# Expert loop of a one-core mixture block: transposes inside the down products, a later dispatch, 2 MB weight transfers

## The reference, cut to what matters

```python
logits = (t @ w_router + b_router)             # t: (512, 1024)
top_val, top_idx = lax.top_k(logits, 4)
gate = jax.nn.softmax(top_val, axis=-1)
# for every expert e, on the tokens routed to it
h = xb @ w_mlp1[e] + b_mlp1[e]                 # (n, 1024) @ (1024, 2048)
glu, lin = jnp.split(h, 2, axis=-1)
glu = jnp.minimum(glu, 7.0)
lin = jnp.clip(lin, -7.0, 7.0)
a = glu * jax.nn.sigmoid(1.702 * glu) * (lin + 1)
y = a @ w_mlp2[e] + b_mlp2[e]                  # (n, 1024) @ (1024, 1024)
out[token] += y * gate                         # then residual and a final RMS norm
```

## Time and profile before

| | |
|---|---|
| median of 3 runs | 1647.25 us (1645.18 to 1649.3) |
| the profiled execution's own time | 1645.66 us |
| its span | 1643.8 us |
| first product of the expert loop | 566.07 us |
| last product of the expert loop | ends at 1610.61 us |
| PE, busy and share of the span | 1437.5 us, 87% |
| DVE, ACT, POOL | 757.7, 546.1, 293.5 us |
| bytes moved | 475.18 MB |

### The profile page before, as it was taken

The page is one execution under the profiler, slowest core; times in us unless marked ns, Lnnn a source line. Parts: engine busy times, 40 slices in busy tenths (PEclk is TensorE's granted clock), DMA queues, the critical chain, the costliest instruction groups (busy, mean ns, idle before and its releaser), DMA issues. The chain is left out here.

```text
span 1643.8 us, 36064 instructions
## 1 busy us (share of the span) xinstructions
PE 1437.5 (87%) x13229; PEld 765.6 (47%) x13230; DVE 757.7 (46%) x1812; ACT 546.1 (33%) x1035; POOL 293.5 (18%) x188
## 2 busy tenths in 40 slices
PE   5899998599997688899999899889889898898981
PEld 2788875366776233344444334333333333343431
DVE  6899976899314623322233233323422422332236
ACT  3432223655323022333223322332342333223323
POOL 4344557411461000000000000000000000000000
PEclk8999998799999699999999999999999999999996
DMA  4223231111329289999999999999999999999995
GB/s 152 77 89 102 90 103 41 37 39 39 106 93 381 96 322 401 411 386 371 373 373 408 404 401 409 396 406 399 413 412 391 412 410 404 409 397 391 404 406 206
DMA packets 78112, 475.18 MB, mean 289 GB/s; under 512 B 11008, under 2 KB 11264, under 8 KB 28928
## 3 DMA queue, kind: packets, MB, share of 16 engines
q1 hardware_dynamic: 69648, 455.72, 70.1%
q0 software_dynamic: 7280, 16.79, 2.9%
q10 hardware_dynamic: 1152, 2.24, 0.4%
HBM read 466.71 MB, written 16.78 MB: 294 GB/s over the span
## 5 line engine op out<-in xcount | busy, mean ns | idle before, releaser
L1033 PE MATMUL bank<-big,ring 128*32 128x512 f32 x4992 | 562.3, 605 | 49.0 <-issue 48.9
L1033 PEld LDWEIGHTS bank<-big,ring 128*32 128x32 f32 x4992 | 156.9, 111 | 420.8 <-issue 419.8
L1055 PE MATMUL bank<-big,mix 128*32 128x256 f32 x4992 | 279.1, 380 | 0.7 <-DMA big<-in_d_w 0.7
L992 ACT ACTIVATE mix<-bank,sgate 32x256 f32<-32x256 f32 x384 | 179.2, 467 | 157.4 <-PE bank L1055 123.8
L1055 PEld LDWEIGHTS bank<-big,mix 128*32 128x32 f32 x4992 | 157.4, 110 | 107.9 <-issue 4.7
L957 POOL DMA_INDIRECT y_rows<-mix,sidx x32 | 30.9, 965 | 914.3 <-ACT mix L992 914.3
L981 ACT ACTIVATE ring<-ring 128x256 f32<-128x256 f32 x96 | 40.1, 417 | 439.4 <-DVE ring L1178 439.4
L1176 DVE TENSOR_TENSOR ring<-bank,b 128x512 f32<-128x512 f32 x96 | 66.1, 688 | 202.7 <-PE bank L1033 196.4
L435 PE MATMUL bank<-mix_r,sm_r 128*128 128x512 f32 x344 | 141.6, 412 | 15.5 <-POOL uT_r L234 10.1
L673 DVE SCALAR_TENSOR_TENSOR bank<-big,chan,bank 128x512 f32<-128x512 f32 x224 | 148.2, 752 | 0.0
L435 PE MATMUL bank<-uT_r,sm_r 128*128 128x512 f32 x344 | 136.6, 397 | 0.0
(11 more groups left out here) (262 smaller groups left out, 1649.7 us busy)
## 6 DMA issues: line engine op xcount, KB each, us to landing
big<-in_d_w SPq DMA_DIRECT2D x384, 1024.0 KB, 16.2
ring<-in_d_dense SPq DMA_DIRECT2D x67, 512.0 KB, 3.3
big<-y_rows SPq DMA_DIRECT2D x2, 2048.0 KB, 22.3
xT<-in_d_xT SPq DMA_DIRECT2D x4, 512.0 KB, 9.3
uT<-in_d_x SPq DMA_DIRECT2D x1, 2048.0 KB, 9.6
u_rows<-xT SPq DMA_DIRECT2D x4, 512.0 KB, 16.6
xT<-y_rows SPq DMA_DIRECT2D x1, 2048.0 KB, 15.9
xT<-y_rows SPq DMA_DIRECT2D x4, 512.0 KB, 5.3
```

Of the source, the lines that this page charges most:

```text
L992: out = act.activation(t.ysb[g * G:(g + 1) * G, c * FC:(c + 1) * FC], bank[PY[g % 2]][token, 0:FC], ACT.Copy, scale=t.sgate[token, bass.ds ...
L1033: mm = pe.matmul(halves(bank[g][c * G:(c + 1) * G, :], FC), t.xe[:, k, g * G:(g + 1) * G], cols, start=(k == 0), stop=(k == KB - 1), tile_ ...
L1055: mm = pe.matmul(bank[PY[g % 2]][c * G:(c + 1) * G, 0:FC], t.aT[:, g, x, b * G:(b + 1) * G], t.w2[:, b, x, c * FC:(c + 1) * FC], start=(b ...
```

## The change

Six things, all in the expert loop.

1. `K_EACH` is 4 instead of 5.
2. `dispatch(i + 1)` and `spread_bias(i)` come after the second chunk of w1 instead of after the first.
3. `turn_act(i, 0)` stands before the last tile's second half of `up` in a three-tile piece, and after `up` in a two-tile piece; `turn_act(i, g + 1)` stands inside `down(i, g)`, after its third quarter.
4. The sequencer's waits with `sem_inc` of two-tile pieces give way to `after(sem)`, a matmul of one column whose end updates the semaphore.
5. DVE turns each tile right after its `swiglu`, and ACT copies the next piece's transposed rows after the second sigmoid instead of after the third.
6. The weights come in transfers of 2 MB: four for w1 and two for w2, each with a row of 16 KB per partition, laid out so in HBM. Chunks are released, and waited for, in pairs. The first expert's weights too.

```diff
-K_EACH = 5
+K_EACH = 4
+PAIRS = KB // 2
...
-                for k in range(KB):
-                    sp.wait_ge(t.s_w1used, i * KB + (k + 1 - KB))
-                    sp.dma_start(t.w1[:, k, :], t.d_w1[bass.ds(e, 1), k * P:(k + 1) * P, :].rearrange("a p n -> (a p) n")).then_inc(t.s_w1[k], 16)
-                for j in range(4):
-                    sp.wait_ge(t.s_w2used, i * 4 + (j - 3))
+                for q in range(PAIRS):
+                    sp.wait_ge(t.s_w1used, i * PAIRS + (q + 1 - PAIRS))
+                    sp.dma_start(t.w1[:, 2 * q:2 * q + 2, :], t.d_w1[bass.ds(e, 1), q].rearrange("e p a n -> (e p) a n")).then_inc(t.s_w1[q], 16)
+                for q in range(2):
+                    sp.wait_ge(t.s_w2used, i * 2 + (q - 1))
...
-                turn(i + 1)
+                    if g == 1:
+                        turn(i + 1)
...
+            def after(sem):
+
+                pe.matmul(bank[5][0:G, 2 * P:2 * P + 1], ident[:, 0:G], ident[:, 0:1], start=True, stop=True).then_inc(sem, 1)
+
...
-                    if g == 0:
-                        pe.wait_ge(t.s_w2[b], i * 16 + 16)
+                    if g == 0 and b % 2 == 0:
+                        pe.wait_ge(t.s_w2[b // 2], i * 16 + 16)
...
+                    if b == 2 and g < last:
+                        turn_act(i, g + 1)
+                        if g + 2 == NG - 1 and last < NG - 1:
+                            after(t.s_at)
...
-                    mm.then_inc(t.s_w1used, 1)
-                    if k == 0:
+                    if k % 2:
+                        mm.then_inc(t.s_w1used, 1)
+                    if k == 1:
                         pe.wait_ge(t.s_slots, i + 1)
                         pe.wait_ge(t.s_ysb, i * NG + 1)
                         dispatch(i + 1)
                         spread_bias(i)
                 for g in range(groups):
+                    if g == NG - 1:
+                        pe.wait_ge(t.s_slots, i + 3)
+                        turn_act(i, 0)
...
                 if groups < NG:
-
-                    pe.wait_ge(t.s_w1used, i * KB + KB)
-                    pe.sem_inc(t.s_up, 1)
-                pe.wait_ge(t.s_slots, i + 2)
-                turn_act(i, 0)
+                    pe.wait_ge(t.s_slots, i + 3)
+                    after(t.s_up)
+                    turn_act(i, 0)
                 turn(i + 1)
-                turn_act(i, 1)
                 down(i, 0, last)
-                if groups == NG:
-                    turn_act(i, 2)
-                else:
-                    pe.wait_ge(t.s_ae, i * NG + 3)
-                    pe.sem_inc(t.s_at, 1)
                 down(i, 1, last)
                 if groups == NG:
                     down(i, 2, last)
                 else:
-                    pe.wait_ge(t.s_w2used, i * 4 + 4)
-                    pe.sem_inc(t.s_y, 1)
+                    after(t.s_y)
...
-                for g in range(2):
+                for g in range(NG):
                     gated(i, g, step, base)
                     swiglu(i, g)
-                turned(i, 0)
-                gated(i, 2, step, base)
-                turn(i + 1)
-                turned(i, 1)
-                swiglu(i, 2)
-                turned(i, 2)
+                    if g == 1:
+                        turn(i + 1)
+                    turned(i, g)
```

More of the change, by code:

```diff
@@ L203, in _ @@
             sp.wait_ge(t.s_merge, 2 * KB)
-            for k in range(KB - 2):
-                sp.dma_start(t.w1[:, k, :], t.d_w1[0, k * P:(k + 1) * P, :]).then_inc(t.s_w1[k], 16)
-            for j in range(4):
-                sp.dma_start(t.w2[:, j, :, :], t.d_w2[0, j]).then_inc(t.s_w2[j], 16)
+            for q in range(PAIRS - 1):
+                sp.dma_start(t.w1[:, 2 * q:2 * q + 2, :], t.d_w1[0, q]).then_inc(t.s_w1[q], 16)
+            for q in range(2):
+                sp.dma_start(t.w2[:, 2 * q:2 * q + 2, :, :], t.d_w2[0, q]).then_inc(t.s_w2[q], 16)
             sp.wait_ge(t.s_prod, used(N_CHUNK - 1))
-            for k in range(KB - 2, KB):
-                sp.dma_start(t.w1[:, k, :], t.d_w1[0, k * P:(k + 1) * P, :]).then_inc(t.s_w1[k], 16)
+            sp.dma_start(t.w1[:, KB - 2:KB, :], t.d_w1[0, PAIRS - 1]).then_inc(t.s_w1[PAIRS - 1], 16)
             for j in range(TT):
@@ L920, in _ @@
                 e = expert_of(sp, i)
-                for k in range(KB):
-                    sp.wait_ge(t.s_w1used, i * KB + (k + 1 - KB))
-                    sp.dma_start(t.w1[:, k, :], t.d_w1[bass.ds(e, 1), k * P:(k + 1) * P, :].rearrange("a p n -> (a p) n")).then_inc(t.s_w1[k], 16)
-                for j in range(4):
-                    sp.wait_ge(t.s_w2used, i * 4 + (j - 3))
-                    sp.dma_start(t.w2[:, j, :, :],
-                                 t.d_w2[bass.ds(e, 1), j].rearrange("e p a n -> (e p) a n")).then_inc(t.s_w2[j], 16)
+                for q in range(PAIRS):
+                    sp.wait_ge(t.s_w1used, i * PAIRS + (q + 1 - PAIRS))
+                    sp.dma_start(t.w1[:, 2 * q:2 * q + 2, :], t.d_w1[bass.ds(e, 1), q].rearrange("e p a n -> (e p) a n")).then_inc(t.s_w1[q], 16)
+                for q in range(2):
+                    sp.wait_ge(t.s_w2used, i * 2 + (q - 1))
+                    sp.dma_start(t.w2[:, 2 * q:2 * q + 2, :, :],
+                                 t.d_w2[bass.ds(e, 1), q].rearrange("e p j a n -> (e p) j a n")).then_inc(t.s_w2[q], 16)
             sp.wait_ge(t.s_scat, last * 16)
@@ L931, in _ @@
                 if r:
-                    sp.wait_ge(t.s_w1used, last * KB + 2 * r)
+                    sp.wait_ge(t.s_w1used, last * PAIRS + r)
                 sp.dma_start(t.early[r], t.d_y4[:, :, r, :]).then_inc(t.s_early[r], 16)
@@ L988, in _ @@
                     else:
-                        act.wait_ge(t.s_w2used, i * 4 + 4)
+                        act.wait_ge(t.s_w2used, i * 2 + 2)
                     for c in range(4):
@@ L1056, in down @@
                                            start=(b == 0 and x == 0), stop=(b == 3 and x == 1), tile_position=(0, c * G))
-                    if g == last:
+                    if g == last and b % 2:
                         mm.then_inc(t.s_w2used, 1)
+                    if b == 2 and g < last:
+                        turn_act(i, g + 1)
+                        if g + 2 == NG - 1 and last < NG - 1:
+                            after(t.s_at)
                 if g < last:
@@ L1065, in work @@
                 for k in range(K_EACH):
-                    pe.wait_ge(t.s_w1[k], i * 16 + 16)
+                    if k % 2 == 0:
+                        pe.wait_ge(t.s_w1[k // 2], i * 16 + 16)
                     for g in range(groups):
                         mm = up(k, g)
-                    mm.then_inc(t.s_w1used, 1)
-                    if k == 0:
+                    if k % 2:
+                        mm.then_inc(t.s_w1used, 1)
+                    if k == 1:
                         pe.wait_ge(t.s_slots, i + 1)
@@ L1075, in work @@
                 for g in range(groups):
+                    if g == NG - 1:
+                        pe.wait_ge(t.s_slots, i + 3)
+                        turn_act(i, 0)
                     for k in range(K_EACH, KB):
-                        if g == 0:
-                            pe.wait_ge(t.s_w1[k], i * 16 + 16)
+                        if g == 0 and k % 2 == 0:
+                            pe.wait_ge(t.s_w1[k // 2], i * 16 + 16)
                         mm = up(k, g)
-                        if g == last:
+                        if g == last and k % 2:
                             mm.then_inc(t.s_w1used, 1)
@@ L1172, in gated @@
                 else:
-                    dve.wait_ge(t.s_w1used, i * KB + KB)
+                    dve.wait_ge(t.s_w1used, i * PAIRS + PAIRS)
                 if g == 0:
@@ L1498, in build @@
         t.s_w = sems("s_w", NSLOT)
-        t.s_w1 = sems("s_w1", KB)
-        t.s_w2 = sems("s_w2", 4)
+        t.s_w1 = sems("s_w1", PAIRS)
+        t.s_w2 = sems("s_w2", 2)
         t.s_early = sems("s_early", TOPK - 1)
@@ L1575, in lay_out @@
         "d_b2": np.tile(a["b_mlp2"][0], (TT, 1)), "d_b1": b1,
-        "d_w1": a["w_mlp1"][0],
-        "d_w2": a["w_mlp2"][0].reshape(E, 4, 2, P, D).transpose(0, 1, 3, 2, 4),
+        "d_w1": a["w_mlp1"][0].reshape(E, PAIRS, 2, P, 2 * D).transpose(0, 1, 3, 2, 4),
+        "d_w2": a["w_mlp2"][0].reshape(E, 2, 2, 2, P, D).transpose(0, 1, 4, 2, 3, 5),
     }
```

## The result

The changed kernel takes 1636.06 us (median of 7, 1633.0 to 1640.05), the kernel before 1645.18 in the same comparison (median of 7, 1641.81 to 1649.3). The ratio is 0.995, interval 0.9937 to 0.9964: faster by 0.5%, about 9 us, where 25 us were forecast. The profiled execution took 1639.19 us, span 1637.4. Its loop runs from 565.3 to 1602.9 us, 1037.6 us instead of 1044.5.

A forecast was written before the change was run, and what follows sets the result against it. TensorE looked like the bound, within about 1% of the transfers' pace, which then caps the gain. First product 566.1, +6.1, stream +998.5, +9.5, rows -5, gather +5, end +6.5 give 1586.7; with 33.2 and 1.9, 1622 us; range 1603 to 1643.

The forecast's parts named there:

- the term of the stream: Expert loop: weights, gather and scatter need 31 x 13.11 = 406.4 MB, 998.5 us at 407 GB/s.
- its idle time in the first piece: Stream in the loop's first piece: 41 us at 283 GB/s carry 28.5 us of work; +9.5 us charged.
- PE's gain: TensorE in the loop: 60 us idle and 10 us half clock go, 9 us of new matmuls come; 983 us alone.
- Larger rows: Weight transfers: 16 KB rows save between nothing and 27 us; 5 us taken.
- The gather behind larger rows: Two-tile pieces, before `turn(i + 1)`: the gather lands later, PE waits 0 to 3.0 us in 18 pieces; 5 us charged.
- The clock: Waits for weights in two-tile pieces bring half clock; up to 24 us in three-tile pieces, 1646 us; nothing charged; chance 0.06.
- Waits for weights: Expected sign in the loop: PE waits for `big<-in_d_w` 25 to 50 us in total instead of 2.
- The second rival: Late gather at full price in two-tile pieces: PE 983 + 54 = 1037 us, time 1638 us; chance 0.12.
- No gain: Stream was the bound already at 32.6 us per piece, 13 us more; later releases 10 us: 1645 us; chance 0.09.
- The stream is no wall: Weight stream: larger rows save their upper bound, 27 us instead of 5, giving 1600 us; chance 0.08.

The follow-up runs named there:

- without a stream: Weight transfers inside the loop cut to 64 bytes per partition: changed kernel 1581.54 us, kernel before 1644.28 us.
- the runs with one strip: One of four column strips computed in up and down, all transfers kept: changed kernel 1629.81 us, kernel before 1637.46 us.

## Why the prediction was wrong

**The step that failed** is the term of the stream, "998.5 us at 407 GB/s", with "its idle time in the first piece, +9.5". With the 5 us each for larger rows and the gather it came to 1008 us from the first issue to the last landing. Measured: 572.5 to 1597.0, 1024.5 us. The mechanism was right, the stream caps PE's gain; the term was too small by 16.5 of the 17.4 us between the sum and the profiled execution. The other 0.9 is small differences at both ends. The parts of the 16.5, worked out from the landings:

- The pace. A piece was put at 32.2 us, from the 407 GB/s of one window of 282.6 us. It is 32.5, of which the weights are 29.5 and gather and scatter 3.0. Over 31 pieces, +9. The 407 already contained gather and scatter, so their price is not what was missed; the window was too short to stand for the loop. In the same trace the last landings of experts 9 to 31 are 32.6 us apart, and a longer window has 404 GB/s, 32.4 us:

```profile
900.00:1550.00 650.00, 591.96 (x6880) 250.69 (x6876) 208.91 (x684) 210.95 (x405) 37.99 (x40) 0.98 1.00 404
```

- The run of three-tile pieces 4 to 7. PE needs 35.8 us there and the single buffer stops the stream; experts 7 to 9 took 36.6, 35.0 and 33.8 us: +8. The prediction says that the late release "costs nothing later as long as there is always a transfer queued", and there was not. With narrow matmuls these 8 us go. With 1 MB transfers they stand elsewhere: experts 7 to 9 take 97.9 us in all, but the first 45.2 and the next two 33.8 and 34.2, and the whole stream 1024.9 us.
- The first expert took 43.2 us, 10.7 over the pace instead of 9.5: +1. The last took 2 less, without gather and scatter in its way.

**Point by point.** *PE's gain*: 60 + 10 - 9 = 61 us predicted, 66.1 of loop and 62.7 of time measured without a stream. Right, and so are its places; two-tile pieces in a row kept 1.1 us before the dispatch, nine times. *Larger rows*: 5 us taken; 4.4 us in the old order, nothing beyond noise in the new one. In the runs with one strip the pace differed by 0.1 us per expert. The price of the row is not separated from that of the release in pairs, which works the other way. *The gather behind larger rows*: predicted landing 8.6 to 13.1 us after issue, measured 12.1; predicted wait 0 to 3.0 us per two-tile piece, measured 1.8 in the mean of 14, 2.7 at most. Charged 5 us; with 1 MB transfers the wait is gone and the time is 1 us less, since PE waits for weights instead. The Trainium skill ("DMA: Bandwidth & Descriptors", Queues, rings and completion order) has engines serve their queues in turn; the landing times agree, nearer the upper figure. *The clock*: it fell where forecast, in starved two-tile pieces (0.90, 28.56 us busy instead of 24.72), and the three-tile pieces after the first kept 1.00. In the loop PE is busy 933 us instead of the 909 without a stream; nothing was charged for it. That fits the stream as the bound, but no run tests the clock by itself. *Waits for weights*: 25 to 50 us predicted, 16.2 measured, 40.2 with 1 MB transfers.

**The rivals.** The second rival's time, 1638 us, is the nearest of all, and by luck: its mechanism, PE held up by the gather at full price, fell, since without that wait (1 MB transfers) the time is the same. "No gain" had the pace right (32.6 us) and was the nearer one in substance, at a chance of 0.09; it missed that PE, not the stream, bounded the kernel before (1644.3 us without a stream). "The stream is no wall" fell most clearly. What would have shown the second part of the miss stood in the trace of before: the slices from 699 to 863 us, the run of three-tile pieces, move 386, 371, 373 and 373 GB/s. I read them as PE holding back the stream before, and charged the new kernel nothing for the same stretch.

Open: why the weight rows take longer beside the gather and not beside the scatter, and so why a gather of about 0.26 MB costs the stream 2.1 us when its bytes are worth 0.6. Gathers with longer rows, or from another place, were not tried. The last microsecond between the two transfer sizes in the new order is within the intervals.

## What to carry to other kernels

When two limits lie within a few per cent, measure each by itself before valuing a change to one: the same kernel with its transfers cut to slivers, and with its matmuls made narrow. Take the pace of a stream from landing to landing over many transfers, not from the rate in one window: 1% of it was over half of this miss. Price a small transfer that shares the engines by what the big stream loses while it runs, not by its bytes. Where pieces differ in length and the buffer is single, the stream stops in the long ones even if it binds on the mean; sum it over runs of pieces, not over the mean.

## What the runs showed of the hardware

- Gather and scatter of together 0.52 MB cost a saturated stream 3.0 us per piece (gather 2.1, scatter 0.9), where their bytes at 427 GB/s are 1.2 us. Beside the gather the weights of an expert occupy the engines for 30.7 us, beside the scatter for 29.7, as without either. Rows skipped by the bounds cost nothing that shows: 427 against 428 GB/s.
- A gather beside weight rows of 8 KB landed after 8.6 us, beside rows of 16 KB after 12.1, with almost no stream after 3.9.
- The stream kept 427 GB/s beside a TensorE busy for 96% of the time, in one strip of four; with rows of 16 KB and of 8 KB its pace per expert was the same within 0.1 us (32.5 and 32.6 in the runs with one strip).
- Four matmuls on different column strips take the time of one: 96 instructions in 10.51 us, 24 in 10.49.
